# Index, queries and tables made one stage earlier, and the prompt's retention norm done for two blocks at a time

## The chip, the cores and the metric

The kernel runs on one core of a Trainium2 chip. The metric is the device time of one execution in microseconds (us). The engines are TensorE (PE; PEld is its loading of weights), VectorE (DVE), ScalarE (ACT), GpSimd (POOL) and SyncE (SP). SP and POOL issue the transfers that matter here; all transfers run on 16 DMA engines.

## The reference

The kernel computes one layer of a decoder step for a prompt of 2048 tokens and for 8 sampled requests. Three kinds of head share one input projection. Of the change's parts this is the core:

```python
def step(S, inp):                       # prompt retention, one chunk of 128 tokens
    qb, kb, vb = inp
    sc = jnp.einsum('bihd,bjhd->bhij', qb, kb) * intra[None]
    o = (jnp.einsum('bhij,bjhe->bihe', sc, vb)
         + jnp.einsum('bihd,bhde->bihe', qb * q_dec[None, :, :, None], S))
    S = S * s_dec[None, :, None, None] + jnp.einsum('bjhd,bjhe->bhde', kb * k_dec[None, :, :, None], vb)
    return S, o
...
def head_norm(o, g):                    # over the 128 values of each head
    mu = jnp.mean(of, axis=-1, keepdims=True)
    var = jnp.mean((of - mu) ** 2, axis=-1, keepdims=True)
    y = ((of - mu) * lax.rsqrt(var + EPS)).reshape(B, T, H * dv)
...
    ckv_past = pool_ckv[page_table].reshape(DB, -1, KV_LORA)     # samples: 128 pages of 128 keys each
    kpe_past = pool_kpe[page_table].reshape(DB, -1, MLA_ROPE)
    s_past = jnp.einsum('bqhc,bkc->bhqk', q_lat, ckv_past) + jnp.einsum('bqhr,bkr->bhqk', q_pe, kpe_past)
```

## The kernel before

The program is six stages with a barrier of all engines between two of them: `project`, `sample_prepare`, `sample_attention_and_retention`, `prompt_latent_prepare`, `prompt_latent_attention`, `merge`. The change touches the second and the third.

`sample_prepare` makes the samples' queries (`q4`), their new retention state (`new_state`), the memory attention's scores (`memory_scores`) and its output. Its tiles are named sp_. SP issues its loads in the order of the code; the loads of `gn` are the last that the semaphore `small` counts, and TensorE starts when `small` is full. TensorE and VectorE then alternate: `outer(b)` (L2487) writes a product, `new_state(b)` (L2332) adds it, `spread(b)` (L2495) spreads a query over the partitions, and `memory_scores(b)` (L2339, L2342) uses it.

`sample_attention_and_retention` does two things at once. Its tiles are named sa_ for the samples' attention and rm_ for the prompt's retention and memory attention. The samples' attention runs in 64 steps g. Per step POOL gathers a 128x4096 tile `nat` (2 MB) and a 128x1024 tile `kp` (0.5 MB) of cache rows by the index table `index`, into one of 4 buffers (`DEEP`); VectorE turns them in three pieces with transposes (`turn(g, n)`, L1811); TensorE forms the scores from `q32` and the turned tiles (`scores(g, n)`, L2039), then `pull_probs` (L2052) and `values` (L2063), which frees the buffer for the gather of step g + 4. The prompt has 16 blocks of 128 tokens; a block begins every 4 steps, and `begun(g, a)` says which block began `a` steps ago. Its parts are woven into the steps in an order that each engine's code writes out. Of block b, the queries and keys are turned (`turn_queries_keys`) at its first step, its retention output is made at its third (`retention_values`, into the PSUM bank `bank_c`, which is half of `bank_m`), and at its fourth VectorE does `new_state`, `head_statistics` and, after `turn(g, 2)`, `head_roots`; ScalarE does `normalise` (L1984) from `bank_c`, TensorE turns the result (`turn_retention`), and at the next step ScalarE scales it with `retention_out` (L1993). The same step then begins block b + 1, whose `turn_queries_keys` waits for `retention_out`. `inverse_root` (L102 to L107) is a chain of 11 operations on tiny tiles, each waiting for the one before.

At the start of this stage SP loads the page table, tables, the queries and the starting maxima (`s_q` and `s_low`, written to memory by the stage before), VectorE lays the queries out in `q32` (L1794) and makes `index` (L1800) with two small TensorE products (L2025, L2027), and only then does POOL issue the first gather.

## Time and profile before

| | us |
|---|---|
| median of 3 runs (lowest to highest) | 2373.36 (2371.57 to 2373.55) |
| time of the profiled execution | 2369.98 |
| its span | 2368.2 |

In the stretch 1000 to 1500 us, which lies wholly within the third stage, TensorE is busy 455.46 us, VectorE 474.44 us and ScalarE 189.44 us, at a granted TensorE clock of 0.99 of full speed. A busy share close to one names a candidate for the bound; the waits of each engine tell whether it is the one that the others wait for. Profile lines give line, engine, operation, output tile and input tiles, and in square brackets the idle time before it with what ended it.

### The profile page before, as it was taken

The page shows a single profiled execution, that of the slowest core. Times are in us where ns is not written, and L with a number is a line of the kernel's source. Part 1 is how long each engine was busy: PE and PEld are TensorE (multiplying, and loading weights), DVE is VectorE, ACT ScalarE, POOL GpSimd, SP SyncE. Part 2 cuts the span into 40 slices and gives each one's busy share as a digit, 9 for nine tenths or more (in the row PEclk, how much of TensorE's full clock was granted, in tenths as well). Part 3 has the DMA queues.
Part 4 walks back from the last instruction along what each step waited for, and adds up shares of the span by engine and source line. Part 5 has one row for each costly group of instructions (what it writes and reads, how often), then busy time and mean ns, then how long its engine had stood idle before and what let it go on. Part 6 is the DMA issues. An engine that isn't in the chain of part 4 may idle for free. (4 is left out here: it accounts for less than half of the span.)

```text
span 2368.2 us, 48459 instructions
## 1 busy us (share of the span) xinstructions
PE 2130.0 (90%) x20401; PEld 1786.1 (75%) x20401; DVE 1299.2 (55%) x2839; ACT 653.1 (28%) x1471; POOL 216.1 (9%) x270
## 2 busy tenths in 40 slices
PE   7899999999999977399999989679599999799998
PEld 6899999987777755277777667558488888668886
DVE  5512444111111116499999989577377777564555
ACT  4311222000100001133334333244244444431110
POOL 0000000000000000122222212010402110000000
PEclk9999999999999985699999999889799999899999
DMA  7322332211121126799999989479997160265452
GB/s 235 112 76 79 97 97 90 81 63 63 63 80 63 53 86 204 284 377 370 371 378 370 365 327 375 148 265 325 253 204 146 43 133 17 81 205 161 142 168 80
DMA packets 183564, 422.20 MB, mean 178 GB/s; under 512 B 15216, under 2 KB 101776, under 8 KB 175160
## 3 DMA queue, kind: packets, MB, share of 16 engines
q0 software_dynamic: 45456, 236.18, 30.3%
q1 hardware_dynamic: 137904, 183.09, 22.9%
q8 instruction: 154, 2.52, 0.4%
q14 instruction: 50, 0.41, 0.1%
HBM read 325.87 MB, written 93.35 MB: 177 GB/s over the span
## 5 line engine op out<-in xcount | busy, mean ns | idle before, releaser
L607 PE MATMUL pj_ps<-pj_wh,pj_xh 128*128 128x256 f32 (+1 forms) x1152 | 326.8, 284 | 2.7 <-issue 2.7
L607 PE MATMUL pj_ps<-pj_wl,pj_xh 128*128 128x256 f32 (+1 forms) x1152 | 323.9, 281 | 0.0
L607 PE MATMUL pj_ps<-pj_wh,pj_xl 128*128 128x256 f32 (+1 forms) x1152 | 323.8, 281 | 0.0
L1811 DVE STREAM_TRANSPOSE sa_turned<-sa_nat 128x2048 f32<-128x2048 f32 x128 | 293.3, 2292 | 19.0 <-DMA sa_kp<-cache_kpe,sa_index 18.7
L505 DVE TENSOR_SCALAR pj_stage<-pj_ps 128x256 f32<-128x256 f32 (+2 forms) x72 | 38.5, 535 | 482.2 <-PE pj_ps L605 314.2
L607 PEld LDWEIGHTS pj_ps<-pj_wh,pj_xh 128*128 128x128 f32 x1152 | 220.2, 191 | 10.6 <-issue 10.1
L2039 PE MATMUL sa_ps_s<-sa_turned,sa_q 128*32 128x128 f32 x5120 | 182.5, 277 | 47.3 <-DVE sa_turned L1811 44.3
L607 PEld LDWEIGHTS pj_ps<-pj_wl,pj_xh 128*128 128x128 f32 x1152 | 220.3, 191 | 0.0
L607 PEld LDWEIGHTS pj_ps<-pj_wh,pj_xl 128*128 128x128 f32 x1152 | 220.1, 191 | 0.0
L605 PE MATMUL pj_ps<-pj_xh,pj_wh 128*128 128x512 f32 x512 | 202.7, 396 | 0.0
L605 PE MATMUL pj_ps<-pj_xl,pj_wh 128*128 128x512 f32 x512 | 201.0, 393 | 0.0
L605 PE MATMUL pj_ps<-pj_xh,pj_wl 128*128 128x512 f32 x512 | 200.9, 392 | 0.0
L2039 PEld LDWEIGHTS sa_ps_s<-sa_turned,sa_q 128*32 128x32 f32 x5120 | 132.3, 110 | 75.4 <-DVE sa_turned L1811 40.0
L398 ACT ACTIVATE pj_stage<-pj_ps 128x256 f32<-128x256 f32 (+2 forms) x72 | 34.0, 472 | 482.3 <-PE pj_ps L605 302.0
L2063 PE MATMUL sa_ps_o<-sa_nat,sa_p_turned 128*16 128x256 f32 x2048 | 129.1, 382 | 13.3 <-issue 12.4
L1225 DVE TENSOR_TENSOR la_pl<-la_ps_p,la_ph 128x512 fp32r<-128x512 f32 (+1 forms) x144 | 88.1, 656 | 81.5 <-ACT la_ph L1254 81.5
L1569 PE MATMUL mg_ps<-mg_wh,mg_ch 128*128 128x512 f32 x384 | 122.7, 401 | 2.9 <-DVE mg_cl L1462 2.6
L1569 PE MATMUL mg_ps<-mg_wl,mg_ch 128*128 128x512 f32 x384 | 121.6, 398 | 0.0
L1569 PE MATMUL mg_ps<-mg_wh,mg_cl 128*128 128x512 f32 x384 | 121.4, 398 | 0.0
L1245 ACT ACTIVATE la_row<-la_row,la_soft 128x128 f32<-128x128 f32 (+7 forms) x64 | 77.2, 1206 | 157.1 <-DVE la_soft L1212 157.1
L605 PEld LDWEIGHTS pj_ps<-pj_xh,pj_wh 128*128 128x128 f32 x512 | 96.1, 188 | 27.8 <-issue 6.9
L605 PEld LDWEIGHTS pj_ps<-pj_xl,pj_wh 128*128 128x128 f32 x512 | 96.1, 188 | 21.8
(379 smaller groups left out, 4084.9 us busy)
## 6 DMA issues: line engine op xcount, KB each, us to landing
pj_raw<-w_in POOLq DMA_DIRECT2D x16, 1024.0 KB, 6.3
s_zn<-pj_stage SPq DMA_DIRECT2D x64, 256.0 KB, 2.1
s_zt<-pj_stage SPq DMA_DIRECT2D x32, 512.0 KB, 2.6
rm_z<-s_zn SPq DMA_DIRECT2D x16, 768.0 KB, 9.4
mg_gate<-s_zt SPq DMA_DIRECT2D x16, 768.0 KB, 6.7
mg_cat<-s_cat SPq DMA_DIRECT2D x16, 768.0 KB, 7.8
pn_x<-x_prompt SPq DMA_DIRECT2D x16, 512.0 KB, 6.3
s_k<-lp_st SPq DMA_DIRECT2D x16, 512.0 KB, 6.4
```

The costliest lines, as they stand in the source:

```text
L398: act.activation(stage_view(n, w_tile), ps[:, n % QUAD, 0:w_tile], ACT.Copy, scale=factor(s)).then_inc(ev_act, 1)
L505: dve.tensor_scalar(stage_view(n, w_tile), ps[:, n % QUAD, 0:w_tile], factor(s), None, ALU.mult).then_inc(ev_dve, 1)
L605: mm = pe.matmul(ps[:, n % QUAD, :], wt[:, k, m * P:(m + 1) * P], of[:, k, c * 512:(c + 1) * 512], **flags)
L607: mm = pe.matmul(ps[:, n % QUAD, 0:w], of[:, k, u * P:(u + 1) * P], wt[:, k, 0:w], **flags)
L1225: dve.tensor_tensor(pl[:, n % RING, 0:w], ps_p[:, n % RING, 0:w], ph[:, n % RING, 0:w], ALU.subtract).then_inc(pl_ok, 1)
L1245: act.activation(row[:, s, q, 0:n], row[:, s, q, 0:n], ACT.Exp, bias=soft[:, s, q, 1:2], scale=MLA_SCALE, accum_out=soft[:, s, q, 2:3]).th ...
L1569: mm = pe.matmul(ps[:, j, n * 512:(n + 1) * 512], a[:, j, c, :], wt[:, c, n * 512:(n + 1) * 512], start=(c == 0 and a is ch and wt is wh), ...
L1811: dve.transpose(turned[:, s, a:z, :, :].rearrange("p c x q -> p x c q"), of.rearrange("p x (c q) -> p x c q", q=QR)).then_inc(t_ok, 1)
L2039: mm = pe.matmul(ps_s[j * QR:(j + 1) * QR, s, 0:TQ * QR], q32[:, u, c, :], turned[:, s, c, j * TQ:(j + 1) * TQ, :].rearrange("p x q -> p ( ...
L2063: mm = pe.matmul(ps_o[j * QR:j * QR + ROWS_Q, 0:KVL], p_turned[:, s, x, j, :], nat[:, g % DEEP, TQ * j + x, :], start=(x == 0), stop=(x == ...
```

## The change

The index table, the query matrix `q32`, the identity, the table `pull` and the starting maxima `low` are held in a new `Keep`, which lives over both sample stages. `sample_prepare` fills them: SP loads the page table and three small tables ahead of `gn`, and after all other loads copies the queries with 16 small transfers from `q4` to `q_in`; POOL clears `q32`; VectorE and TensorE make the index between their other work, and VectorE writes `q32` after `head_norm`. The transfers of `q4` and `low` to memory and back are gone. In the next stage POOL issues the first two gathers at once, the third after the first block's loads and the fourth after the stage's tables; SP issues the first block's loads first.

The retention output of each block is copied from `bank_c` to `kept` by a new ScalarE copy, `keep_out`. `head_statistics` reads the copy, `head_roots`, `normalise`, `turn_retention` and `retention_out` run only for odd blocks and then treat two blocks, the first over `bank_c` and the second over `bank_b`.

```diff
-        pages = r.sb("pages", [STEPS, GP], I32)
-        pages_f = r.sb("pages_f", [STEPS, GP])
-        pagesT = r.sb("pagesT", [GP, STEPS])
-        spread = r.sb("spread", [GP, P])
-        sub = r.sb("sub", [P, 1])
-        index = r.sb("index", [P, STEPS], I32)
-        ident = r.sb("ident", [P, P])
+        index, q32, ident, pull, low = keep.index, keep.q32, keep.ident, keep.pull, keep.low
...
-                        sp.dma_start(q_in[i * QR:(i + 1) * QR, s, :, :],
-                                     t["s_q"][:, s * HEADS * DEC:(s + 1) * HEADS * DEC].rearrange("(k c) n -> c k n", c=QR))\
-                          .then_inc(consts, 16)
...
-                    sp.wait_ge(cat_r_ok, b + 1)
-                    sp.dma_start(t["s_cat"][b, :, 0:W3], cat_r[:, :, :].rearrange("p h q -> p (h q)")).then_inc(cat_r_out, 16)
+                    if b % 2 == 1:
+                        sp.wait_ge(cat_r_ok, b + 1)
+                        for x in range(2):
+                            sp.dma_start(t["s_cat"][b - 1 + x, :, 0:W3], cat_r[:, x, :, :].rearrange("p h q -> p (h q)"))\
+                              .then_inc(cat_r_out, 16)
 
                 load(0)
+                sp.wait_ge(acc_clear, 1)
+                for i in range(QUADS):
...
-                pool.wait_ge(index_ok, 1)
                 for g in range(STEPS):
+                    if g == 2:
+                        pool.wait_ge(z_in[0], 32)
+                    elif g == 3:
+                        pool.wait_ge(m_consts, 16 * M_CONSTS)
...
-                dve.wait_ge(consts, 16 * CONSTS)
-                dve.tensor_copy(pages_f[:, :], pages[:, :]).then_inc(pages_ok, 1)
-                dve.wait_ge(q_clear, 1)
-                for u in range(SETS):
-                    for i in range(QUADS):
-                        b = u * QUADS + i
-                        part = slice(i * QR, (i + 1) * QR)
-                        last = dve.tensor_copy(q32[part, u, :, i * HEADS:(i + 1) * HEADS],
-                                               q_in[part, :, :, :].rearrange("p s k (h b) -> p (s k) h b", b=DEC)[:, :, :, b])
-                last.then_inc(q_ok, 1)
-                dve.wait_ge(index_ps, 1)
-                dve.tensor_copy(pagesT[:, :], ps_s[0:GP, 0, 0:STEPS]).then_inc(pages_ok, 1)
-                dve.wait_ge(index_ps, 2)
-                dve.tensor_scalar(index[:, :], ps_s[:, 1, 0:STEPS], float(SUB), sub[:, :], ALU.mult, ALU.add).then_inc(index_ok, 1)
-                dve.wait_ge(acc_in, 16 * QUADS)
...
+                    dve.wait_ge(kept_ok, b + 1)
                     for h in range(HEADS):
-                        last = dve.bn_stats(stats[:, h, :], bank_c[:, h, :])
+                        last = dve.bn_stats(stats[:, h, :], kept[:, b % 2, h, :])
                     link(last)
+                    if b >= 2 and b % 2 == 0:
+                        dve.wait_ge(root_ok, b // 2)
                     for h in range(HEADS):
-                        last = dve.bn_aggr(mean_var[:, h, :], stats[:, h, :])
-                    link(last)
-                    link(dve.tensor_scalar(var[:, :], mean_var[:, :, 1], EPS, None, ALU.add))
+                        last = dve.bn_aggr(mean_var[:, b % 2, h, :], stats[:, h, :])
+                    last.then_inc(stat_ok, 1)
 
                 def head_roots(b):
-                    if b >= 1:
-                        dve.wait_ge(normed_ok, b)
-                    inverse_root(dve, link, var[:, :], root[:, :], tmp[:, :])
-                    dve.scalar_tensor_tensor(shift[:, :], mean_var[:, :, 0], -1.0, root[:, :], ALU.mult, ALU.mult)\
+                    dve.wait_ge(stat_ok, b + 1)
+                    link(dve.tensor_scalar(var[:, :, :], mean_var[:, :, :, 1], EPS, None, ALU.add))
+                    if b >= 2:
+                        dve.wait_ge(normed_ok, b - 1)
+                    flat = [x[:, :, :].rearrange("p x h -> p (x h)") for x in (var, root, tmp)]
+                    inverse_root(dve, link, *flat)
...
+                def keep_out(b):
+                    act.wait_ge(out_ps, b + 1)
+                    if b >= 2:
+                        act.wait_ge(normed_ok, 2 * (b // 2))
+                    act.copy(kept[:, b % 2, :, :], bank_c).then_inc(kept_ok, 1)
                 def normalise(b):
-                    act.wait_ge(root_ok, b + 1)
-                    if b >= 1:
-                        act.wait_ge(rT_ps, b)
-                    for h in range(HEADS):
-                        last = act.activation(normed[:, h, :], bank_c[:, h, :], ACT.Identity, bias=shift[:, h:h + 1],
-                                              scale=root[:, h:h + 1])
-                    last.then_inc(normed_ok, 1)
+                    act.wait_ge(root_ok, b // 2 + 1)
+                    act.wait_ge(kept_ok, b + 1)
+                    if b >= 2:
+                        act.wait_ge(rT_ps, b - 1)
+                    for x in range(2):
+                        for h in range(HEADS):
+                            last = act.activation(normed[:, x, h, :], kept[:, x, h, :], ACT.Identity, bias=shift[:, x, h:h + 1],
+                                                  scale=root[:, x, h:h + 1])
+                        last.then_inc(normed_ok, 1)
 
                 def retention_out(b):
-                    act.wait_ge(rT_ps, b + 1)
-                    if b >= 1:
-                        act.wait_ge(cat_r_out, 16 * b)
-                    for h in range(HEADS):
-                        last = act.activation(cat_r[:, h, :], bank_b[:, h, :], ACT.Copy, scale=gain[:, h:h + 1])
-                    last.then_inc(cat_r_ok, 1)
-                act.wait_ge(m_consts, 16 * M_CONSTS)
+                    if b == 1:
+                        act.wait_ge(m_consts, 16 * M_CONSTS)
+                    else:
+                        act.wait_ge(cat_r_out, 16 * (b - 1))
+                    for x, bank in enumerate((bank_c, bank_b)):
+                        act.wait_ge(rT_ps, b + x)
+                        for h in range(HEADS):
+                            last = act.activation(cat_r[:, x, h, :], bank[:, h, :], ACT.Copy, scale=gain[:, h:h + 1])
+                        last.then_inc(cat_r_ok, 1)
                 for g in range(STEPS + 2):
...
+                        keep_out(begun(g, 3))
                         memory_turned(begun(g, 3), 0)
                     if begun(g, 4) is not None:
                         memory_out(begun(g, 4))
-                        retention_out(begun(g, 4))
+                        if begun(g, 4) % 2 == 1:
+                            retention_out(begun(g, 4))
...
-                        pe.wait_ge(cat_r_ok, b)
+                        pe.wait_ge(state_ok, b)
+                        pe.wait_ge(cat_r_ok, 2 * (b // 2))
...
-                        pe.wait_ge(normed_ok, b)
+                        pe.wait_ge(kept_ok, b)
+                        pe.wait_ge(cat_r_ok, 2 * (b // 2))
...
-                    pe.wait_ge(normed_ok, b + 1)
+                    pe.wait_ge(kept_ok, b + 1)
                     pe.wait_ge(state_ok, b + 1)
-                    for h in range(HEADS):
-                        mm = pe.transpose(bank_b[:, h, :], normed[:, h, :], ident[:, :])
-                    mm.then_inc(rT_ps, 1)
-                pe.wait_ge(m_consts, 16 * M_CONSTS)
+                    for x, bank in enumerate((bank_c, bank_b)):
+                        pe.wait_ge(normed_ok, b + x)
+                        for h in range(HEADS):
+                            mm = pe.transpose(bank[:, h, :], normed[:, x, h, :], ident[:, :])
+                        mm.then_inc(rT_ps, 1)
...
+class Keep:
+    def __init__(self, nc, ctx):
+        def sb(name, shape, dt=F32):
+            return ctx.enter_context(nc.sbuf_tensor(f"keep_{name}", shape, dt))
+        self.index = sb("index", [P, STEPS], I32)
+        self.q32 = sb("q32", [P, SETS, 3 * QUADS, QR])
+        self.ident = sb("ident", [P, P])
+        self.pull = sb("pull", [P, QUADS, QUADS * ROWS_Q])
+        self.low = sb("low", [P, 2, SETS])
...
+                for u in range(SETS):
+                    sp.dma_start(pages[u * PER_SET:(u + 1) * PER_SET, :].rearrange("s (i k) -> s i k", i=QUADS),
+                                 t["page_table"][u * QUADS:(u + 1) * QUADS, :].rearrange("i (s k) -> s i k", k=PAGES_SEEN))\
+                      .then_inc(pages_in, 16)
...
+                for to, of in ((steps[:, :], t["c_spread"]), (sub[:, :], t["c_sub"]),
+                               (keep.pull[:, :, :].rearrange("p i n -> p (i n)"), t["c_pull"])):
+                    sp.dma_start(to, of).then_inc(pages_in, 16)
...
+                sp.wait_ge(q4_ok, 2)
+                for k in range(QUADS):
+                    for i in range(QUADS):
+                        sp.dma_start(q_in[i * QR:(i + 1) * QR, :, k, :],
+                                     q4[k * QR:(k + 1) * QR, :, :, :].rearrange("p s h b -> p s (h b)")).then_inc(queries_in, 16)
...
+                dve.wait_ge(pages_in, 16 * (SETS + 3))
+                dve.tensor_copy(pages_f[:, :], pages[:, :]).then_inc(pages_ok, 1)
                 dve.wait_ge(mk_in, 16)
                 for b in range(3):
                     memory_scores(b)
                     new_state(2 * b + 2)
                     new_state(2 * b + 3)
+                    if b == 0:
+                        dve.wait_ge(index_ps, 1)
+                        dve.tensor_copy(pagesT[:, :], bank[6][0:GP, 0:STEPS]).then_inc(pages_ok, 1)
+                    elif b == 1:
+                        dve.wait_ge(index_ps, 2)
+                        dve.tensor_scalar(index[:, :], bank[6][:, P:P + STEPS], float(SUB), sub[:, :], ALU.mult, ALU.add)\
+                           .then_inc(pages_ok, 1)
                 for b in range(3, 6):
                     memory_scores(b)
                 head_norm()
+                dve.wait_ge(q_clear, 1)
+                dve.wait_ge(queries_in, 16 * QUADS * QUADS)
+                for u in range(SETS):
+                    for i in range(QUADS):
+                        part = slice(i * QR, (i + 1) * QR)
+                        last = dve.tensor_copy(q32[part, u, :, i * HEADS:(i + 1) * HEADS],
+                                               q_in[part, :, :, :].rearrange("p s k (h b) -> p (s k) h b", b=DEC)[:, :, :, u * QUADS + i])
+                last.then_inc(q32_ok, 1)
...
+                pe.wait_ge(low_ok, 1)
+                pe.wait_ge(pages_ok, 1)
+                pe.transpose(bank[6][0:GP, 0:STEPS], pages_f[:, :], ident[0:STEPS, 0:STEPS]).then_inc(index_ps, 1)
                 for n in range(3):
                     outer(2 * n + 2)
                     outer(2 * n + 3)
+                    if n == 0:
+                        pe.wait_ge(pages_ok, 2)
+                        pe.matmul(bank[6][:, P:P + STEPS], steps[:, :], pagesT[:, :], start=True, stop=True).then_inc(index_ps, 1)
...
```

POOL's order of transfers at the start of the attention stage stays as it was, without the wait for the index ahead of the first gather; the two copies of `q4` and `low` to memory are gone from the stage before. On SP, at the start of the attention stage, this stands in the program before the change (`rm_mkT` to `rm_gain` are the prompt part's tables, `rm_z` and `rm_mq` a block's loads):

```order
L1715 DMA sa_sub<-c_sub 128x1
L1715 DMA sa_ident<-c_ident 128x128
L1715 DMA sa_fold<-c_fold 128x64
L1715 DMA sa_pull<-c_pull 128x256
L1715 DMA sa_low<-s_low 128x2
L1715 DMA sa_w_uv<-w_uv 128x2x512
L1718 DMA sa_q_in<-s_q 32x4x32 x12
L1725 DMA sa_acc<-s_acc 4x2x258 x4
L1731 DMA rm_mkT<-s_mkT 128x1024
```

and this in the changed program, from the preparation's tables to the first loads of the attention stage:

```order
L2287 DMA sp_pages<-page_table 32x4x4 x2
L2292 DMA sp_steps<-c_spread 16x128
L2292 DMA sp_sub<-c_sub 128x1
L2292 DMA keep_pull<-c_pull 128x256
L2294 DMA sp_gn<-ret_gn_g 8x128 x4
L2296 DMA sp_state<-state_ret 128x32x128
L2298 DMA sp_mem_k<-cache_mem_k 128x16x512
L2300 DMA sp_mem_v<-cache_mem_v 128x16x512
L2305 DMA sp_q_in<-sp_q 32x3x32 x16
L2271 UNCONDITIONAL_BRANCH
L1694 UNCONDITIONAL_BRANCH
L1704 DMA rm_z<-s_zn 128x1536
```

Five transfers now stand ahead of `gn` and 16 behind `mem_v`; the attention stage begins with the first block's loads (the two branches are the ends of the stages' code).

On ScalarE, at the last step of a block and the first of the next, this stands there before the change, for every block (`sa_ratio` and `sa_probs` are the samples' exponentials, `sa_p_turned` the copy of their turned shares):

```order
L1970 COPY rm_probsT<-rm_bank_m 128x512
L1934 COPY sa_p_turned<-sa_ps_p 128x256
L1970 COPY rm_probsT<-rm_bank_m 128x512
L1984 ACTIVATE rm_normed<-rm_bank_m,rm_shift,rm_root 128x128 x4
L1925 ACTIVATE sa_ratio<-sa_low 128x1
L1926 ACTIVATE sa_probs,sa_total<-sa_ps_s,sa_low 128x128
L1977 COPY rm_cat_m<-rm_bank_a 128x512
L1993 ACTIVATE rm_cat_r<-rm_bank_b,rm_gain 128x128 x4
L1934 COPY sa_p_turned<-sa_ps_p 128x256
```

and in the changed program, for an odd block:

```order
L1957 COPY rm_kept<-rm_bank_m 128x512
L1944 COPY rm_probsT<-rm_bank_m 128x512
L1908 COPY sa_p_turned<-sa_ps_p 128x256
L1944 COPY rm_probsT<-rm_bank_m 128x512
L1967 ACTIVATE rm_normed<-rm_kept,rm_shift,rm_root 128x128 x8
L1899 ACTIVATE sa_ratio<-keep_low 128x1
L1900 ACTIVATE sa_probs,sa_total<-sa_ps_s,keep_low 128x128
L1951 COPY rm_cat_m<-rm_bank_a 128x512
L1980 ACTIVATE rm_cat_r<-rm_bank_m,rm_gain 128x128 x4
L1980 ACTIVATE rm_cat_r<-rm_bank_b,rm_gain 128x128 x4
L1908 COPY sa_p_turned<-sa_ps_p 128x256
```

For an even block the rows of L1967 and L1980 are absent. `keep_out` stands in front of the first copy of the turned memory probabilities, and in odd blocks eight activations stand where four did, twice.

## Rows read from the trace of the kernel before

**Rows 1.** The page's first line: span of the profiled execution.

```profile
span 2368.2 us, 48459 instructions
```

**Rows 2.** Stretch: from:to, length, busy PE, PEld, DVE, ACT, POOL, granted clock, DMA share, GB/s.

```profile
1000.00:1500.00 500.00, 455.46 (x9850) 352.07 (x9854) 474.44 (x849) 189.44 (x622) 111.52 (x120) 0.99 0.95 365
```

**Rows 3.** Who VectorE waited for, 1000 to 1500 us.

```profile
DVE rm_state L1854 <- PE rm_bank_m L2109: 7.0, 3, 3.4
DVE sa_turned L1811 <- DMA sa_kp<-cache_kpe,sa_index: 4.2, 5, 2.3
DVE rm_bias L1838 <- PE rm_bank_m L2085: 4.0, 8, 0.7
```

**Rows 4.** Timeline from the stage's first issue to the first transpose; last row: gathers to landing.

```profile
954.77 0.81 SPq L1707 DMA_DIRECT2D sa_pages<-page_table  x2
969.49 1.02 POOL L1775 DMA_INDIRECT sa_nat<-cache_ckv,sa_index  x1 [18.53 <-DVE sa_index L1800]
982.88 4.50 DVE L1811 STREAM_TRANSPOSE sa_turned<-sa_nat 128x2048 f32<-128x2048 f32 x2 [13.67 <-DMA sa_kp<-cache_kpe,sa_index]
DMA to landing us min/median/max: 8.6/10.1/21.6
```

**Rows 5.** Timeline rows of the preparation, and two of the next stage's start.

```profile
880.21 1.60 SPq L2279 DMA_DIRECT2D sp_gn<-ret_gn_g  x4
887.73 0.39 PEld L2515 LDWEIGHTS sp_bank<-sp_ident,sp_cqn 8*128 8x128 f32 x3 [17.14 <-DMA sp_gn<-ret_gn_g]
910.68 1.91 PE L2495 MATMUL sp_bank<-sp_zs,sp_one_row 8*128 8x512 f32 x2
910.92 0.88 DVE L2332 SCALAR_TENSOR_TENSOR sp_state<-sp_state,sp_bank 128x128 f32<-128x128 f32 x4 [0.76 <-PE sp_bank L2487]
966.27 1.64 DVE L1794 COPY sa_q<-sa_q_in 32x48 f32<-32x48 f32 x8
968.20 0.68 PE L2027 MATMUL sa_ps_s<-sa_pagesT,sa_spread 16*128 16x64 f32 x2 [1.44 <-DVE sa_pagesT L1798]
```

**Rows 6.** Timeline, VectorE, from the variance to the next step's transpose.

```profile
1239.46 0.17 DVE L1864 TENSOR_SCALAR rm_var<-rm_mean_var 128x4 f32<-128x4 f32 x1
1240.83 0.13 DVE L102 TENSOR_SCALAR rm_tmp<-rm_var 128x4 int32<-128x4 int32 x1
1243.05 2.31 DVE L1811 STREAM_TRANSPOSE sa_turned<-sa_nat 128x2048 f32<-128x2048 f32 x1
```

**Rows 7.** Timeline of the same block: last row of retention_values, new_state, a ScalarE copy.

```profile
1236.67 0.39 PE L2109 MATMUL rm_bank_m<-rm_state,rm_qT 128*128 128x128 f32 x2
1237.34 0.87 DVE L1854 SCALAR_TENSOR_TENSOR rm_state<-rm_state,rm_bank_b 128x128 f32<-128x128 f32 x4
1240.25 0.58 ACT L1970 COPY rm_probsT<-rm_bank_m 128x512 f32<-128x512 f32 x1 [1.08 <-PE rm_bank_m L2119]
```

**Rows 8.** Timeline, the block boundary behind it.

```profile
1243.16 1.50 ACT L1984 ACTIVATE rm_normed<-rm_bank_m,rm_shift,rm_root 128x128 f32<-128x128 f32 x4 [2.33 <-DVE rm_shift L1870]
1245.72 0.29 ACT L1925 ACTIVATE sa_ratio<-sa_low 128x1 f32<-128x1 f32 x1 [1.05 <-DVE sa_low L1819]
1246.73 1.16 ACT L1993 ACTIVATE rm_cat_r<-rm_bank_b,rm_gain 128x128 f32<-128x128 f32 x4
1247.88 1.08 PE L2039 MATMUL sa_ps_s<-sa_turned,sa_q 128*32 128x128 f32 x32 [0.67 <-DVE sa_turned L1811]
1248.89 0.66 PE L2073 MATMUL rm_bank_a<-sa_ident,rm_z 128*128 128x128 f32 x4
1253.26 1.99 PE L2085 MATMUL rm_bank_m<-rm_mkT,rm_mq 128*128 128x256 f32 x8
1255.30 1.23 DVE L1838 TENSOR_REDUCE rm_bias<-rm_bank_m 128x4 f32<-128x1024 f32 x1 [0.67 <-PE rm_bank_m L2085]
```

**Rows 9.** A line's group (PSUM source), and a timeline row (SBUF only).

```profile
L1859 DVE BATCH_NORM_STATS2 rm_stats<-rm_bank_m 128x6 f32<-128x128 f32 x64 | 14.1, 281 | 0.0
934.05 0.28 DVE L2351 TENSOR_TENSOR sp_ret_g<-sp_ret_n,sp_gn 32x128 f32<-32x128 f32 x1
```

128 lines of the change are left out of this document (59 added, 69 removed).

## The prediction

> **What bounds the kernel now.** The span is 2368.2 us [rows 1], the profiled execution 2369.98 us; the stages run one after the other, so a microsecond saved on the path inside a stage is a microsecond of the whole. I read the stretches first. From 1000 to 1500 us VectorE is busy 474.44 of 500 us, TensorE 455.46, and the DMA engines' mean share is 0.95 [rows 2]: three candidates. Then the waits. VectorE waited only 7.0, 4.2 and 4.0 us in its three largest groups: for the retention product, for a gather, and for the memory scores [rows 3]. These and the busy time account for nearly all of the 500 us. VectorE therefore sets the pace, and TensorE and the gathers follow closely behind; what VectorE saves is worth its full price only as far as these two can follow.
>
> The second place is the head of the attention stage. SP issues its first load at 954.77, POOL its first gather at 969.49, and VectorE's first transpose starts at 982.88, after 13.67 us of waiting for that gather [rows 4]. In these 28.1 us the stage does nothing else of weight.
>
> **The head.** After the change POOL waits for nothing, and I put the first gather at the opening of the stage, about 0.1 us behind SP: 969.49 - 954.9 = 14.6 us sooner. From its issue to the first transpose it took 13.4 us; the fastest of the 64 gathers landed in 8.6 and the median in 10.1 us [rows 4]. The first one shared the engines with all of the prompt part's loads. Now two loads stand ahead of those tables and the gather starts beside them, so I take 12.4, 1.0 us better, with bounds from 8.6 (4.8 better) to 2 us worse. The third gather waits for the first block's loads and the fourth for the tables. They are needed two and three steps later, and a step lasts about 8 us (the 64 steps take more than the 500 us of that stretch), so I cost these waits at nothing; the cover is those 16 us of transposes, and if it fails the third or fourth step waits some microseconds. With SP's tables and `w_uv` behind them nothing else is late: they are used at the end of the first step and in the tail.
>
> **The preparation pays.** Four terms. First, five transfers on SP stand ahead of `gn`, at 1.60 / 4 = 0.40 us each 2.0 us, and TensorE's first work waited 17.14 us for `gn` [rows 5]. But `gn` was issued by 881.81 and used at 887.73, so it also queued behind earlier loads, which hides part of a later issue; I take 1.0 (bounds 0.3 and 2.0). Second, the index product. TensorE waits there for VectorE's copy, which stands behind `new_state`: that ended at 910.92 + 0.88 = 911.80, the copy is small (1.64 / 8 = 0.2), the product's row is 0.68 [rows 5], so `spread`, which started at 910.68, starts near 912.7: 2.0 us late. VectorE waits for TensorE all along there (0.76 us before that `new_state`), so this passes on (bounds 1.0 and 2.7). Third, the first turn of the page table on TensorE, less than that product: 0.4. Fourth, the eight copies to `q32`, 1.64 us [rows 5], in a run of VectorE operations that has no wait: 1.6. The 16 query copies have from the end of `mem_v`'s issue until after `head_norm`; that covers them, and without the cover VectorE would wait there. POOL's clearing of `q32` lies in its wait for the first result. Sum 5.0, bounds 3.3 to 6.7.
>
> **VectorE's saving.** Per block the variance takes 0.17 and the chain of roots lasts from 1240.83 to the next transpose at 1243.05, 2.22 us [rows 6]; its tiles are tiny, so twice the width costs as much. Eight of sixteen go: 8 x 2.39 = 19.1 us. `keep_out` is new on ScalarE. It can start when the product ends at 1237.06, a copy of that size takes 0.58, so it ends near 1237.7, while VectorE is in `new_state` until 1238.21 [rows 7]: `head_statistics` waits for nothing. Where `new_state` itself waited for the product [rows 3], the copy also fits beside it. Without that cover it would cost 0.6 us a block. Behind it on ScalarE stands the copy of the turned memory probabilities, which now ends near 1238.3; the next such copy, which follows TensorE's use of the first, starts at 1240.25 [rows 7].
>
> Whether the statistics get faster is open: they read SBUF now. The row from PSUM is 281 ns, and an operation as wide from SBUF alone took 0.28 us [rows 9], so the sum has nothing for it. The Trainium skill, "VectorE: DVE Perf Modes", section "The TRN2 errata", gives VectorE a fixed part of 120 cycles with a PSUM source and 58 without; at 0.96 GHz that would be 65 ns for each of 64, 4.1 us more gained. The same section gives ScalarE 224 cycles from SBUF against 172 from PSUM, 43 ns at 1.2 GHz for each of the 64 activations of `normalise`, an estimate of 2.8 us against the change if all lay on the path. The rows show no such difference for VectorE, and none here pairs ScalarE's.
>
> **What TensorE gives back after even blocks.** VectorE now comes 2.39 us sooner to its reduction of the memory scores. In the block shown it already waited 0.67 us there, for the product that ran from 1253.26 [rows 8]. TensorE gets there sooner only by four transposes (0.66, as the row of the same kind) and by a wait for the tiles that falls away (0.67) [rows 8]: 1.3 us. So 1.1 us of the 2.4 turns into a wait; since the wait now is 4.0 us over 16 blocks [rows 3], some blocks have slack, and I take 1.0 x 8 = 8 us. Bounds: nothing, and all of the 19.1.
>
> **After odd blocks.** `normalise` goes from 4 to 8 activations, at 1.50 / 4 = 0.38 until 1243.16 + 3.0 = 1246.2. The exponentials and the memory copy take 1.0 (1245.72 to 1246.73), `retention_out` 8 x 0.29 = 2.3: end at 1249.5, where TensorE's `turn_queries_keys`, which waits for it, started at 1248.89 [rows 8]. It is 0.6 us late, and behind it in TensorE's order stand the last scores of the step, `values` (which frees a gather's buffer) and the memory scores. I take 0.4 of it as reaching VectorE, 8 x 0.4 = 3.2 us. Bounds: nothing, and the whole of the added activations, 8 x 2.7 = 21.6.
>
> **The gathers.** With shorter steps they are waited for more often than the 5 times and 4.2 us now [rows 3]; I add 1 us (0 to 6).
>
> **Sum.** -14.6 - 1.0 + 5.0 - 19.1 + 8.0 + 3.2 + 1.0 = -17.5 us: 2369.98 becomes 2352.5. The median of the runs is 3.4 above that execution, so 2355.9, and I say 2356.
>
> **Rivals.** (1) TensorE follows: its lag at the boundaries finds slack, and the saving is kept whole. For it: the waits are short and many blocks show none. Against: TensorE is busy 455 of 500 us. -14.6 - 1.0 + 5.0 - 19.1 = -29.7, time 2343.7. (2) TensorE or the gathers take all of the saving, and only the head stays: -10.6, time 2362.8. For it: both shares in rows 2. Against: in most blocks VectorE waited for neither. (3) The head falls short: the third and fourth gathers, held back until the loads have landed beside two gathers, come late and VectorE loses 6 us there; -17.5 + 6 = -11.5, time 2361.9. For it: a gather took up to 21.6 us in this crowd [rows 4]. (4) Slower: the double work after odd blocks holds TensorE's order, `values` frees buffers late, and the gather that follows is late for its transpose. It decides from the point where an odd boundary costs (29.7 - 9 + 4.7) / 8 = 3.2 us; at 4 us the time is 2373.4 - 20.7 + 32 = 2385. Against it: only 0.6 us is on the path by the rows, and 2.7 us is all that is added.
>
> **Chances and range.** Forecast 0.48; (1) 0.20, (2) 0.16, (3) 0.08, (4) 0.05, something else 0.03. The forecast's own range, from its bounds nearest the rows, is 2349 to 2361. The range of 2343 to 2366 reaches over (1), (2) and (3) and leaves out (4). About 0.2%, 4.7 us, is what a measurement of this kernel tells from no change. Every case but (4) lies beyond it on the fast side, with a tail of the second and third that does not: faster 0.88, same 0.07, slower 0.05.
>
> **What would show it.** In the profile after: the first gather within 0.3 us of the stage's opening; that opening near 959.8; the first transpose near 972; half as many root chains; VectorE's waits for the memory scores up from 4 to some 12 us, in blocks that follow even ones; ScalarE's copy done before the statistics are due. The prediction is wrong if VectorE waits long for `kept`, if the transposes wait for gathers by more than 10 us behind the first four steps, or if the preparation grows by more than 7 us.

## The result, and the profile after

The changed kernel took 2381.28 us, median of 10 runs (2375.14 to 2387.36), against 2371.76 us for the kernel before on the same chip (10 runs, 2362.70 to 2379.31): ratio 1.0039, 95% interval 1.0024 to 1.0053. It is 9.5 us slower, where 17.5 us faster (2356 us) was forecast. Its profiled execution took 2377.07 us.

The span, and the stretch from 1000 to 1500 us (columns as in [rows 2]):

```profile
span 2375.3 us, 48408 instructions
```

```profile
1000.00:1500.00 500.00, 461.83 (x9795) 356.46 (x9797) 454.30 (x739) 195.64 (x624) 112.20 (x120) 0.99 0.95 362
```

VectorE's work did fall, from 474.44 to 454.30 us of the 500; no time came of it. Who it waited for in the same stretch, against [rows 3]:

```profile
DVE sa_turned L1776 <- DMA sa_kp<-cache_kpe,keep_index: 15.4, 13, 2.7
DVE sa_negated L1784 <- PE sa_ps_s L2020: 9.4, 4, 4.3
DVE rm_bias L1805 <- issue: 6.2, 8, 1.4
DVE rm_state L1823 <- PE rm_bank_m L2094: 4.2, 7, 1.9
DVE sa_acc L1798 <- PE sa_ps_o L2044: 2.5, 3, 2.0
DVE rm_bias L1805 <- PE rm_bank_m L2070: 2.1, 2, 1.4
```

The waits for gathers went from 4.2 to 15.4 us, and the wait for the step's scores (`sa_negated`) from 1.6 to 9.4 us.

The head of the stage, rows of the timeline that answer to [rows 4], then the rows that undo it:

```profile
960.72 0.36 SPq L1704 DMA_DIRECT2D rm_z<-s_zn  x1
961.50 1.01 POOL L1756 DMA_INDIRECT sa_nat<-cache_ckv,keep_index  x1 [4.05 <-POOLq L85]
974.48 4.51 DVE L1776 STREAM_TRANSPOSE sa_turned<-sa_nat 128x2048 f32<-128x2048 f32 x2 [12.30 <-DMA sa_kp<-cache_kpe,keep_index]
989.73 0.94 POOL L1756 DMA_INDIRECT sa_nat<-cache_ckv,keep_index  x1 [20.95 <-DMA rm_gain<-ret_gn_g]
993.40 1.22 DVE L1805 TENSOR_REDUCE rm_bias<-rm_bank_m 128x4 f32<-128x1024 f32 x1 [6.41 <-PE rm_bank_m L2070]
```

The first transpose starts at 974.48 in place of 982.88, 8.4 us sooner. The tables are whole only near 989.6 us; the fourth gather and the first memory product stand behind them, and VectorE waits 6.41 us. By the fifth step (step 4) 5.1 of the 8.4 us are left: 1011.36 against 1016.50.

The chain after an odd block, at step 24, in the timeline of the changed kernel (answers to [rows 8]):

```profile
1182.22 3.19 ACT L1967 ACTIVATE rm_normed<-rm_kept,rm_shift,rm_root 128x128 f32<-128x128 f32 x8 [2.22 <-DVE rm_shift L1845]
1185.46 0.66 PE L2122 MATMUL rm_bank_b<-keep_ident,rm_normed 128*128 128x128 f32 x4 [0.82 <-ACT rm_normed L1967]
1186.05 1.08 PE L2020 MATMUL sa_ps_s<-sa_turned,keep_q 128*32 128x128 f32 x32
1187.32 1.13 ACT L1980 ACTIVATE rm_cat_r<-rm_bank_b,rm_gain 128x128 f32<-128x128 f32 x4
1188.60 0.63 PE L2055 MATMUL rm_bank_a<-keep_ident,rm_z 128*128 128x128 f32 x4
```

TensorE stands 0.82 us for the second half of the scales, and the step's first scores start at 1186.05, 3.94 us behind the step's transpose (1182.11); in the kernel with the copy alone (below) it is 2.63 us. At step 17, the second step behind block 3, it is worse:

```profile
1117.07 0.42 ACT L1908 COPY sa_p_turned<-sa_ps_p 128x256 f32<-128x256 f32 x1
1120.16 1.12 PE L2055 MATMUL rm_bank_a<-keep_ident,rm_z 128*128 128x128 f32 x4 [3.04 <-issue]
1123.21 0.35 DVE L1784 CUSTOM_DVE_ANT_0 sa_negated<-sa_ps_s,sa_none,keep_low 128x128 f32<-128x128 f32 x1 [4.31 <-PE sa_ps_s L2020]
```

ScalarE's outputs were done by 1117.3, yet TensorE's transposes wait until 1120.16, 3.04 us in all and for nothing the profile names, and VectorE 4.31 us behind them.

The tail. After the last block ScalarE has twice the scales, then twice the outputs ahead of the copy that the last values need:

```profile
1512.81 3.19 ACT L1967 ACTIVATE rm_normed<-rm_kept,rm_shift,rm_root 128x128 f32<-128x128 f32 x8 [2.27 <-DVE rm_shift L1845]
1517.91 1.13 ACT L1980 ACTIVATE rm_cat_r<-rm_bank_b,rm_gain 128x128 f32<-128x128 f32 x4
1518.91 0.39 ACT L1908 COPY sa_p_turned<-sa_ps_p 128x256 f32<-128x256 f32 x1
1519.36 3.52 PE L2044 MATMUL sa_ps_o<-sa_nat,sa_p_turned 128*16 128x256 f32 x32 [2.06 <-ACT sa_p_turned L1908]
1533.50 0.33 SPq L1742 DMA_DIRECT2D s_cats<-sa_cats  x1
```

The same two of the kernel before:

```profile
1516.17 1.92 PE L2063 MATMUL sa_ps_o<-sa_nat,sa_p_turned 128*16 128x256 f32 x32 [0.96 <-ACT sa_p_turned L1934]
1528.05 0.33 SPq L1764 DMA_DIRECT2D s_cats<-sa_cats  x1
```

TensorE waits 2.06 us, not 0.96, and the values then take 3.52 us, not 1.92.

The stage can be cut at VectorE's first transpose of steps 0, 4, 44 and 60 and at the issue that stores `s_cats`. The table has these stretches of each kernel's profiled execution (differences of start times), and the ratio to before over all its runs (each kernel beside runs of before on the same chip; the chips differ between groups of kernels). The stretches come from one execution of each kernel, and the executions of one kernel lie up to 17 us apart (those of before above), so a few microseconds in one column show little by themselves. The profile of before has two blocks of 37.8 and 37.6 us (steps 44 to 52) where its others have 31.6 to 33.6, with a pause of TensorE of 3.69 us in one; the four unpaired kernels without a further edit to the gathers show 455.5 to 458.1 us for steps 4 to 60, so its 463.3 makes it look some 7 us too slow there. The column 4 to 44 is free of that.

| kernel | ratio, 95% | step 4 at | 4 to 44 | 4 to 60 | 60 to store |
|---|---|---|---|---|---|
| before | 1 | 1016.5 | 324.1 | 463.3 | 48.2 |
| after | 1.0039 (1.0024, 1.0053) | 1011.4 | 334.2 | 468.4 | 53.7 |
| e1 first half | 0.9976 (0.9962, 0.9990) | 1016.6 | 325.8 | 457.0 | 48.9 |
| e2 pairing alone | 1.0049 (1.0036, 1.0063) | 1017.5 | 342.7 | 475.2 | 56.0 |
| e3 gain load apart | 1.0036 (1.0023, 1.0049) | 1012.8 | 338.0 | 477.0 | 55.4 |
| e4 roots left out | 0.9993 (0.9978, 1.0007) | 1017.9 | 327.4 | 458.1 | 48.7 |
| e6 before, fewer gathers | 0.9959 (0.9944, 0.9975) | 1018.9 | 321.8 | 448.7 | 48.4 |
| e7 after, fewer gathers | 0.9995 (0.9981, 1.0008) | 1010.5 | 325.4 | 454.6 | 56.3 |
| e8 copy alone | 1.0005 (0.9991, 1.0019) | 1016.0 | 326.5 | 455.5 | 48.9 |
| e9 pairing, roots back | 1.0084 (1.0060, 1.0107) | 1021.2 | 336.8 | 468.8 | 53.0 |
| e10 after, 5 buffers | 1.0044 (1.0029, 1.0058) | 1012.6 | 333.6 | 469.1 | 53.0 |
| e11 first half, 5 buffers | 0.9986 (0.9969, 1.0003) | 1013.3 | 329.2 | 466.3 | 48.6 |
| e12 after, copy first | 1.0012 (0.9997, 1.0026) | 1012.5 | 340.3 | 472.0 | 49.3 |
| e13 e11, copy first | 0.9986 (0.9974, 0.9998) | 1015.7 | 331.4 | 466.5 | 47.8 |
| e14 staggered pairs | 0.9992 (0.9976, 1.0009) | 1011.7 | 330.8 | 465.8 | 52.4 |
| e15 e14, copy first | 0.9974 (0.9954, 0.9994) | 1010.3 | 332.6 | 466.6 | 52.6 |
| e16 e1, copy first | 0.9973 (0.9960, 0.9987) | 1015.8 | 325.0 | 455.6 | 47.7 |
| e17 e4, fewer gathers | 0.9925 (0.9907, 0.9942) | 1020.0 | 316.0 | 442.7 | 48.5 |
| e18 e15, fewer gathers | 0.9924 (0.9907, 0.9940) | 1015.3 | 320.0 | 448.6 | 49.6 |
| e19 e16, no hold | 1.0018 (1.0003, 1.0033) | 1017.8 | 329.5 | 459.9 | 48.2 |

### The profile page after: what moved, and what is told of

Same layout as the page of the kernel before. It is cut to its first block and busy times, and to the rows that moved or that the text cites. A ratio compares the mean times of both kernels' runs of the same rounds, so it can differ in the third digit from the quotient of the medians.

```text
span 2375.3 us, 48408 instructions
## 1 busy us (share of the span) xinstructions
PE 2145.5 (90%) x20401; PEld 1797.1 (76%) x20401; DVE 1282.4 (54%) x2734; ACT 664.2 (28%) x1487; POOL 216.3 (9%) x269
## 3 DMA queue, kind: packets, MB, share of 16 engines
q1 hardware_dynamic: 137680, 183.02, 22.8%
## 5 line engine op out<-in xcount | busy, mean ns | idle before, releaser
L607 PEld LDWEIGHTS pj_ps<-pj_wh,pj_xh 128*128 128x128 f32 x1152 | 220.4, 191 | 10.6 <-issue 10.1
L2020 PE MATMUL sa_ps_s<-sa_turned,keep_q 128*32 128x128 f32 x5120 | 179.7, 277 | 29.0 <-DVE sa_turned L1776 28.6
L2020 PEld LDWEIGHTS sa_ps_s<-sa_turned,keep_q 128*32 128x32 f32 x5120 | 134.2, 110 | 51.0 <-DVE sa_turned L1776 34.4
```

The source lines that it names most:

```text
L607: mm = pe.matmul(ps[:, n % QUAD, 0:w], of[:, k, u * P:(u + 1) * P], wt[:, k, 0:w], **flags)
L2020: mm = pe.matmul(ps_s[j * QR:(j + 1) * QR, s, 0:TQ * QR], q32[:, u, c, :], turned[:, s, c, j * TQ:(j + 1) * TQ, :].rearrange("p x q -> p ( ...
```

## The experiments

**The two halves.** e1 is the changed kernel with the per-block norm of before; e2 is the kernel before with the changed norm, store and their waits. The diff between the two norms is that of the change, so it is not shown again.

> Only the first half of the change (index, query matrix and tables in the preparation), with the head norm block by block as before. Theory A (the pairing loses the time): the gain that the two profiles show at step 4, 1016.50 to 1011.36, is kept through the 64 steps and the tail: 5 us faster than before, ratio 0.998. Theory B (the head and the preparation lose it, +5.6 us before the stage opens and the slow gain load behind which the fourth gather stands): no faster than before, ratio 1.000 to 1.004.

> Only the second half (the head norm for two blocks at a time from a copy), with the preparation and head of before. Theory A: the whole loss and the lost gain of the head are here: steps 4 to 60 about 5 us longer and the tail about 5 us longer, 10 us slower, ratio 1.004. Theory B: ratio 0.995 to 1.000.

Theory A holds. The first half gains 0.0024, 5.7 us; the pairing costs 0.0049, 11.6 us; their sum is 6 us, the change 9.5, which the intervals allow. Every kernel with a pairing that doubles the work and all gathers has 333.6 us or more in steps 4 to 44, every unpaired one with all gathers and four buffers 324.1 to 329.5.

**The load of the gains.** In e3 it has its own semaphore, behind all other loads:

```
-        M_CONSTS = 5
+        M_CONSTS = 4
+                sp.dma_start(gain[:, :], ...).then_inc(gain_in, 16)     # after load(1), fold and w_uv
-                        act.wait_ge(m_consts, 16 * M_CONSTS)            # retention_out, b == 1
+                        act.wait_ge(gain_in, 16)
```

> The changed kernel with the 4-byte-element load of the gains at the end of SyncE's loads and on a semaphore of its own, so that neither the fourth gather nor the first memory product waits for it. If this load costs the head the 21 us wait of the fourth gather: the gather goes out some 10 us earlier, step 4 opens 5 us or more earlier than 1011.36, and the time is 4 to 6 us under that of the changed kernel (ratio to before 1.001 to 1.002) if the steps behind it keep it. If the four gathers land at the rate of the DMA engines whatever their order, it is within 1 us of the changed kernel.

The fourth gather, in its timeline:

```profile
990.85 0.94 POOL L1756 DMA_INDIRECT sa_nat<-cache_ckv,keep_index  x1 [20.25 <-DMA rm_state<-c_zero]
```

It stands as long as in the changed kernel (20.25 against 20.95 us), now for another table, and the time differs by 0.0003, less than 1 us: the load of 4-byte elements is not to blame. The last table lands some 25 us behind its issue in both (issued at 966.31 and 965.05).

**The hold.** e19 is e16 (below) without GpSimd's two waits, which order transfers and guard no data:

```
                 for g in range(STEPS):
-                    if g == 2:
-                        pool.wait_ge(z_in[0], 32)
-                    elif g == 3:
-                        pool.wait_ge(m_consts, 16 * M_CONSTS)
```

> The first half of the change with the last copy first, and GpSimd's two waits (for the first block's loads ahead of the third gather, for the tables ahead of the fourth) taken out, which only order transfers. The four gathers go out one behind another as before the change. If the hold is what costs the head its gain, step 4 opens 3 to 6 us earlier and the time is 3 to 5 us under the same kernel with the hold (ratio to before 0.995 to 0.996). If the first gathers and loads share one throughput, the tables and the first block then land later by as much, and it stays at 0.997 to 0.998.

Both missed. It is slower than e16 by 0.0045, 10.7 us. VectorE waits twice as long for the memory scores, whose tables are now loaded beside four gathers (timeline, e19 and then e16, which holds two of them back):

```profile
997.30 1.22 DVE L1797 TENSOR_REDUCE rm_bias<-rm_bank_m 128x4 f32<-128x1024 f32 x1 [12.52 <-PE rm_bank_m L2042]
```

```profile
995.71 1.23 DVE L1801 TENSOR_REDUCE rm_bias<-rm_bank_m 128x4 f32<-128x1024 f32 x1 [5.95 <-PE rm_bank_m L2046]
```

TensorE's product for these scores waits in both for the last table, the gains: issued at 962.50 it is there for 993.60 in e19, 31 us later, and in e16 25 us later (967.12 and 992.10). In the profile step 4 opens only 1.9 us later than in e16, but e19's preparation had started 4.4 us sooner in that execution and the stage opened 4.6 us sooner (958.10 against 962.68). From the opening to step 4 it takes 59.7 us against 53.2, 6.5 us more, which is the longer wait. With 4.5 us more in steps 4 to 44 that makes 11.0 us; why those steps are longer I did not settle.

**What the saved roots are worth.** e4 saves them with no pairing (blocks 2, 4, ... 14 use an older root), e9 gives them back to the pairing on tiles that nobody reads:

```
+                    if b == 0 or b % 2 == 1:                            # e4, in head_roots
                         inverse_root(dve, link, var[:, :], root[:, :], tmp[:, :])
+                    if begun(g, 3) is not None and begun(g, 3) % 2 == 0:  # e9, beside head_roots
+                        inverse_root(dve, link, spare[:, 0, :], spare[:, 1, :], spare[:, 2, :])   # and variance, shift
```

> The kernel before, with the eleven instructions of the inverse root left out after blocks 2, 4, ... 14 (their scales are those of an earlier block), 7 times 2.2 us of VectorE, with no copy and no doubled work. If VectorE sets the pace of the 64 steps, 15 us faster (ratio 0.9935). If the gathers' transfers do (the DMA engines are 96% busy over these steps), 0 to 4 us faster, ratio 0.998 to 1.000, with the waits for gathers grown from 1.9 us. If TensorE follows only in part, 7 to 10 us.

> The kernel with the pairing alone, in which VectorE does after each even block a root of 4 columns again, on tiles that nobody reads, so that its saving of 8 times 2.4 us is gone and the doubled work after odd blocks stays. If VectorE's time after even blocks counts for nothing, within 3 us of the pairing alone (ratio 1.004 to 1.006). If the pairing alone saves it and loses it elsewhere, 12 to 19 us slower than it, ratio 1.010 or more. A third way: it is faster than the pairing alone, if a VectorE that comes too soon after even blocks is itself what brings the disorder.

Without 15.4 us of VectorE's work e4 is 1.7 us faster (interval 5.2 faster to 1.7 slower). e9's median, 2387.2 us, is beside e2's 2386.4; by ratio it is 8 us slower, between what the two theories expect. What the roots are worth inside the pairing is therefore known only as 0 to 8 us. Where the saving goes shows step by step. Mean time from one step's first transpose to the next, over groups of eight steps from step 8 (six or seven of each), by the step's place in its group (3 holds the even block's norm, 7 the odd one's):

| place | 1 | 3 | 4 | 5 |
|---|---|---|---|---|
| before | 7.91 | 11.71 | 6.43 | 8.17 |
| e8 copy alone | 7.53 | 11.15 | 6.36 | 8.04 |
| e4 roots left out | 7.64 | 9.17 | 7.36 | 9.15 |
| after | 9.31 | 8.72 | 8.24 | 8.54 |
| e9 pairing, roots back | 9.69 | 11.38 | 6.54 | 7.85 |
| e14 staggered | 7.96 | 9.59 | 7.47 | 9.18 |

The 11.71 of before holds one step of 16.49 us (step 51, in one of the two odd blocks named above); its other six are 10.85 to 11.01, mean 10.91. Against these, place 3 gains 1.7 us in e4 and 2.2 after the change, and places 4 and 5 give back 1.9 and 2.2: all of it. At place 5 the gather is not there: in e4 and in the changed kernel VectorE waits 0.4 to 2.7 us for it in six and in five of the six groups, with the roots back (e9) in one. After the change:

```profile
1277.41 2.27 DVE L1776 STREAM_TRANSPOSE sa_turned<-sa_nat 128x2048 f32<-128x2048 f32 x1
1286.42 2.31 DVE L1776 STREAM_TRANSPOSE sa_turned<-sa_nat 128x2048 f32<-128x2048 f32 x1 [2.63 <-DMA sa_kp<-cache_kpe,keep_index]
```

**Buffers.** e10 and e11 have five gather buffers in place of four. e10 makes room by letting `normed` lie in `cat_r` and by loading `w_uv` over `mv` at the end.

```
-DEEP = 4
+DEEP = 5
```

> The changed kernel with five gather buffers in place of four (room for the fifth: the normalised rows lie where the finished ones go, and the last weights are loaded over the memory values at the end). If the saved roots are lost because the gather for the second step after an even block is issued only when TensorE has finished with its buffer and needs 10 to 13 us to land, this takes the wait away: VectorE's waits for gathers fall from 15.4 us to under 4, and the time is 6 to 11 us under the changed kernel's (ratio to before 0.999 to 1.001). If the DMA engines' throughput is the limit, a further buffer changes nothing (1.003 to 1.005).

> The first half of the change alone with five gather buffers. Its waits for gathers are 3.8 us in the 64 steps with four, so by the first theory 1 to 4 us faster than the first half alone (ratio to before 0.996 to 0.997); by throughput, the same as it, 0.9976.

The waits for gathers are gone in both, and nothing is won. e11 is the clean case (nothing but `DEEP` differs from e1); in e10 the shared tile also makes `normalise` wait for the store of the pair before. In e10, VectorE's waits from 1020 to 1480 us:

```profile
DVE rm_bias L1806 <- PE rm_bank_m L2072: 11.9, 14, 1.4
DVE rm_state L1824 <- PE rm_bank_m L2096: 9.7, 10, 3.3
DVE sa_negated L1785 <- PE sa_ps_s L2022: 9.6, 5, 4.4
```

It waits for TensorE instead. TensorE's own pauses without a visible releaser ("issue") sum to 31.3 us in that stretch in e10 (24.2 in the changed kernel), and to 23.5 in e11 (13.1 in e1), 22.8 in e13 (13.1 in e16). So the gather wait was the nearest limit, with TensorE close behind it.

**Transfers.** In e6 (on before) and e7 (on after) every fourth step is computed on the rows that its buffer got once: 22% fewer bytes, DMA share 0.78 and 0.76 in place of 0.96 and 0.95.

```
+                        if g % DEEP == DEEP - 1:
+                            continue
                         pool.wait_ge(pv_ps, g - DEEP + 1)
...
-                        dve.wait_ge(nat_in[k], 32 * (g // DEEP + 1))
+                        dve.wait_ge(nat_in[k], 32 * (g // DEEP + 1) if k < DEEP - 1 else 32)
```

> The kernel before, in which every fourth step is computed on the rows that the fourth buffer got once, so that a quarter of the gathers (14 of the 64 pairs behind the first four, some 22% of the bytes of the 64 steps) is left out. If the DMA engines, 96% busy here, set the pace, VectorE takes over: its 438.6 us of work in the 463.3 us leave at most 25 us, 10 to 25 us faster than before (ratio 0.990 to 0.996). If they do not, the waits for gathers of before (1.9 us) are all that is saved: ratio 0.999.

> The changed kernel with the same gathers left out. If the DMA engines are what keeps VectorE's saved 19 us from counting, the order of the two kernels turns: this one is 5 to 20 us faster than the kernel before with fewer gathers. If the pairing costs by its own waits (doubled ScalarE and TensorE work after odd blocks), it stays as much slower than that kernel as the changed kernel is than before, 5 to 10 us.

e6 is 9.7 us faster than before, at the edge of the 10 to 25 us expected if the transfers set the pace. The order does not turn: the changed kernel stays 8.5 us slower (0.0036). So the pairing costs by its own waits, which the transfers do not explain. e17 and e18 add the same edit to e4 and e15.

> The kernel before with a quarter of the gathers left out and with the inverse root left out after blocks 2, 4, ... 14 (7 times 2.2 us). With the fewer gathers alone the time was 0.9959 of before, with VectorE 448 of 460 us busy and its waits under 5 us. If the transfers swallow the saved roots, they are worth 8 to 15 us now: ratio 0.990 to 0.9925. If TensorE does, 0 to 4 us: 0.994 to 0.996.

> Paired roots with the other work one block per boundary and the last copy first, with a quarter of the gathers left out. If transfers swallow the saving: ratio 0.989 to 0.992, under the first half's 5 us and the fewer gathers' 10 us together (0.994). If TensorE does: 0.993 to 0.995.

With fewer transfers the roots left out are worth 0.0034, 8 us of 15.4, against 0.0007 with all of them. That points to the transfers for about half of what is swallowed; the difference of the two, 0.0027, is about as large as its uncertainty, so it isn't shown. e18, at 0.9924, ties with e17 and lies between what its two theories expect.

TensorE's pauses without a visible releaser, summed from 1020 to 1480 us, fall with the transfers in all four pairs: 17.0 us in before and 10.4 in e6, 17.3 in e4 and 6.5 in e17, 25.6 in e15 and 11.8 in e18, 24.2 in the changed kernel and 20.0 in e7. So "TensorE follows" and "the transfers follow" are not two separate limits here: fewer transfers also took pauses from TensorE. What joins them no run shows.

**The copy.** e8 is before with `keep_out`, statistics and scales from its copy, nothing paired.

> The kernel before with ScalarE's copy of the retention output to memory alone, from which statistics and scale are taken block by block; nothing is paired. If the loss is the pairing's, this stays within 2 us of before (ratio 0.999 to 1.001). If the copy itself (0.6 us on ScalarE at each of 16 boundaries, with VectorE behind it) is what holds the steps, 5 us or more slower.

No cost of it can be told from the runs: 1.0005, that is 2.1 us faster to 4.5 slower.

**The tail.** In e12, e13 and e16 (on after, e11 and e1) the last step's copy goes first:

```
                     if begun(g, 4) is not None:
+                    # ahead of it: if g == STEPS: copy_probs(g - 1), and the later call for g < STEPS only
                         memory_out(begun(g, 4))
```

> The changed kernel in which ScalarE copies the last step's turned probabilities ahead of the last pair's memory and retention output, not behind them. In the changed kernel's trace TensorE waits 2.06 us for this copy and the values behind it take 3.52 us in place of 1.92. If the doubled work in the tail is what costs 5 us there, the tail gives back 3 to 5 us of it (ratio to before 1.002); if the tail's 5 us are chance of one profile, nothing (1.004).

> The first half of the change alone, with five gather buffers and with ScalarE's last copy of the turned probabilities ahead of the last outputs. The last values start up to 1.7 us earlier than in the same kernel without it: ratio to before 0.995 to 0.9965 if both help, 0.9976 if neither does.

> The first half of the change alone, with four gather buffers, and the last copy of the turned probabilities ahead of the last outputs of one block. In the trace of the first half alone TensorE waits 0.96 us for this copy; up to 1.2 us faster than it: ratio to before 0.997 to 0.998, not to be told from the first half alone.

e12 is 0.0027, 6.4 us, faster than the changed kernel. Its last values:

```profile
1522.21 1.92 PE L2046 MATMUL sa_ps_o<-sa_nat,sa_p_turned 128*16 128x256 f32 x32 [0.49 <-ACT sa_p_turned L1908]
```

They take 1.92 us again, and the stretch behind step 60 is 49.3 us, against 53.7. In all six kernels with doubled work and the old order (after, e2, e3, e7, e9, e10) the values take 3.25 to 3.61 us behind a wait of 2.06 or 2.07; in before, e1, e4, e8 and e11 1.92 behind 0.96. The 5.5 us of the changed kernel's tail against before are 0.9 in the last steps, 2.3 by which the values start later behind the last step's first transpose (17.4 against 15.1 us), 1.6 in the values themselves and 0.7 behind them.

In kernels without doubled work the same edit is worth nothing that can be told: e16 0.9973 beside e1's 0.9976, e13 0.9986 as e11.

**One block at a boundary.** e14 keeps the paired roots and the copy, but scales, turns and puts out block b-1 at the boundary of block b, one block at each (15 with 14 at the end):

```
+        def done(b):
+            return [] if b == 0 else [b - 1] if b < BLOCKS - 1 else [b - 1, b]
-                        if begun(g, 3) % 2 == 1:
-                            normalise(begun(g, 3))
+                        for s in done(begun(g, 3)):
+                            normalise(s)                # turn_retention, retention_out, store alike
```

> The changed kernel with the roots still taken for two blocks at once, but scale, transposes and output of one block at each boundary, a block late (block 15's with block 14's at the end). If the doubled work that stands together after odd blocks is what costs inside the 64 steps (some 1.4 us in the second step behind each odd block, and TensorE's 3 us stalls at steps 17 and 41), it goes away: 5 to 10 us under the changed kernel (ratio to before 1.000 to 1.002), the tail's 5 us still in it. If it is the copy and the late order as such, it stays at 1.003 to 1.005.

> The kernel before this one with ScalarE's last copy of the turned probabilities ahead of the last outputs. The tail's 4 to 6 us come back: ratio to before 0.998 to 0.999 by theory D, the same as the first half alone, since the saved roots by themselves are worth 2 us. Below 0.996 the saved roots would be worth more than measured with the roots left out.

e14 is 0.0047, 11 us, faster than the changed kernel, with the same roots saved. Place 1 is back from 9.31 to 7.96 us. Those 9.31 us are a mean of unequal steps. The long pauses before `rm_bank_a` at steps 17 and 41, which every kernel with doubled work shows (1.2 to 5.0 us each; only one of the two in e7 and e10), make these two steps 12.64 and 10.77 us long, 4.1 and 2.2 more than before, while at the other five the change costs 0.3 to 1.0. In e14 both pauses are gone, with one of 1.8 us left at step 17. TensorE's unexplained pauses as a whole are not fewer (26.5 us against 24.2); they stand elsewhere. Its last values show that a long wait ahead of them is not enough to slow them, for they wait about as long as in the changed kernel:

```profile
1517.51 1.92 PE L2047 MATMUL sa_ps_o<-sa_nat,sa_p_turned 128*16 128x256 f32 x32 [2.00 <-ACT sa_p_turned L1912]
```

e15 is 0.0018, 4 us, faster than e14, which the intervals do not tell from nothing. In its profile the values start 1.5 us sooner behind the last step, but the three steps from 60 to 63 are 1.5 us longer, so the stretch behind step 60 stays at 52.6 us. e15 ties with e1 and e16: pairing, even so, wins nothing over the first half alone. The best versions are e16 and e15, 2366.67 and 2366.11 us, 5 to 6 us under before and 15 under the change; e16 is the simpler one.

## Why the prediction was wrong

**The preparation pays**: right by this profile. The stage opens 5.95 us later, of which 0.32 was there at the preparation's start: 5.6 against 5.0. `gn` was waited for 1.2 us longer (18.30 against 17.14, forecast 1.0). But the term varies. From the issue of `sp_rot` to the stage's opening the changed kernel takes 83.3 us, the twelve other kernels with its preparation 82.5 to 85.3; before, e4, e6 and e17 take 77.6 to 77.9, and e2, e8 and e9, with the same preparation as before, 81.0 to 81.5, for no reason that I found. In e1 the preparation costs 7.4 us, above the bound of 6.7.

**The head**: the first transpose came 8.4 us sooner, forecast 10.6; the gather went out 0.8 us behind the opening, not 0.1, and needed 13.0 us to the first transpose, not 12.4. The step that failed is "I cost these waits at nothing". The four steps take 36.9 us to 33.6 before, with the 6.41 us wait for the first memory scores in them, and in e1 38.9: a cost of 3.3 and 5.3 us. Over its runs the first half alone is worth 5.7 us (2.4 to 9.0), not 10.6. Its one profile doesn't show even that much: step 4 opens at 1016.6 us, as before. Rival (3) had about the size, but not the cause: without the hold it is worse (e19). There the fourth gather went out 21 us sooner after the opening, and the last table came 31 us behind its issue in place of 25. The DMA engines were 0.96 busy from 961 to 1017 us in the changed kernel, 0.93 in e16 and 0.87 in e19.

**VectorE's saving, and what TensorE gives back after even blocks**: the work went as forecast (20.1 us less), and the cover for the copy held (e8). The step that failed is "I take 1.0 x 8", with "I add 1 us" for the gathers. e4 measures the saving at 1.7 us of 15.4, so nearly all is given back, by the gather of the second step behind the block, and with a buffer more by TensorE. Rival (2) was the right one for this term. Rows 3 showed few and short waits (16 of them, 15.2 us of 500, the longest 3.4), and I read that as slack; with TensorE, VectorE and the transfers 91 to 96% busy there was hardly any to take. Of the signs of being wrong that I had named, one showed: VectorE's transposes wait 15.4 us for gathers, where I had set 10.

**After odd blocks**: mis-sized. "0.4 of it as reaching VectorE", 3.2 us in all, became 9.8 us over seven boundaries in the profile (place 1, 7.91 to 9.31 us), and e14, which undoes the doubling at each boundary, is 11 us faster. I priced the lateness of one TensorE instruction, and not the scores of the step, which stand behind the second block's transposes and start 1.3 us later; with that go the 0.3 to 1.0 us at five of the boundaries. The rest, 6.4 us, lies at steps 17 and 41 with their pauses of 3.0 and 2.1 us, for which no term could stand. Rival (4) named the doubled work after odd blocks, but had it act through gathers that come late; behind it VectorE waits for scores (4.31 us), and the gathers that it waits for stand behind even blocks. A boundary costs 1.4 us on average, under the 3.2 of that rival; it was enough, since the saving that it was set against did not exist.

**The tail** has no term in the sum. The last pair's doubled outputs stand ahead of the copy for the last values: 53.7 against 48.2 us.

**The statistics' source**: of the two rules that I weighed from the Trainium skill, "VectorE: DVE Perf Modes", section "The TRN2 errata", the one for VectorE does not show here, and the one for ScalarE does in part. Groups of lines, 955 to 1540 us, before and then after:

```profile
L1984 ACT ACTIVATE rm_normed<-rm_bank_m,rm_shift,rm_root 128x128 f32<-128x128 f32 x64 | 24.1, 456 | 38.0 <-DVE rm_shift L1870 38.0
```

```profile
L1829 DVE BATCH_NORM_STATS2 rm_stats<-rm_kept 128x6 f32<-128x128 f32 x64 | 13.9, 280 | 0.0
L1967 ACT ACTIVATE rm_normed<-rm_kept,rm_shift,rm_root 128x128 f32<-128x128 f32 x64 | 25.5, 481 | 18.2 <-DVE rm_shift L1845 18.2
```

VectorE's statistics take 280 ns from SBUF and 281 from PSUM [rows 9], so the 65 ns of that rule are absent. ScalarE's scales take 481 ns from SBUF and 456 from PSUM, 25 ns more, where the rule gives 43.

From the parts: -5.7 for the first half, 11 after odd blocks, 5 in the tail, -1.7 for the roots make 8.6 us, against 9.5 measured. The 11 us hold some of the tail too (e14's values are short again, 52.4 against 53.7 us behind step 60). e15, which has both edits, lies 15.4 us under the changed kernel, which makes the sum 8.0.

**What stays open**: what TensorE's pauses at steps 17 and 41 are, which make up most of what the doubled work costs inside the steps, and why pauses fall with fewer transfers; how far transfers and how far TensorE swallow the roots; where e1 gains what its profile doesn't show; and why steps 4 to 44 are longer in e19.

## What to carry to other kernels

Where TensorE, VectorE and the transfers are each 91 to 96% busy, as in the kernel before from 1020 to 1480 us, work taken from one of them is worth little until it has been measured; leaving the work out altogether (one run) prices it before any rewriting. Doing two blocks' work at once saves fixed costs on one engine and doubles the burst on the others: look at what stands behind the burst in their order, spread it one block at a time, and look at the last step by itself. Short waits on all sides beside such busy shares were a sign of balance here, and not of slack.
